# A transformer block pair on one core: the triangular inversion keeps one running matrix, and GpSimd's weight remainders come in two halves

## Chip, core and metric

The kernel runs on one core of a Trainium2 chip. What is measured is the time of one launch on the device, in microseconds (us). Before the change the median of three runs is 1421.59 us (1421.49 to 1422.59).

## What is computed

Two transformer blocks follow each other on a sequence of 512 tokens and 1024 features, in float32. The part that the change touches is in the first block: a gated delta rule, in chunks. The reference has chunks of 64; the kernel works in four chunks of 128 tokens and four heads, which is mathematically the same. Per chunk and head it needs the inverse of a unit lower triangular matrix:

```
lower = where(causal_strict, (k * beta) @ k.T * decay, 0)
tmat  = inverse(eye + lower)
u, w  = tmat @ (v * beta), tmat @ (k * beta * exp(gc))
```

The other part is in every dense product of both blocks (`w_in`, `w_out`, gate, up, down and so on): weights and activations are float32, and each product is made of reduced-precision pieces, as the next section says.

## The kernel before

**Dense products.** A weight block of 128 x 1024 values (`WB`) is loaded by the SP queue into one of three `raw` buffers. ScalarE casts it to the rounded high part `wh` (line 2128), and GpSimd subtracts, `wl = raw - wh`, in one instruction of 128 x 1024 (line 1780), which raises `wl_ready` by one. A product tile is `gemm` (lines 1794 to 1825): per 128 rows of weights, called a k below, three matmuls of 128 x 512: high weight by high activation (1818), low by high (1819), high by low (1820). `gemm` waits for the block's `wl_ready` before its first matmul. `gemm_pair` and `gemm_triple` work on two and three tiles at once (lines 1827 to 1871), and `by_token` (line 953, through `pe_tile`) does products by token; all wait for `wl_ready` too, and so does SP before it loads a `raw` buffer again (line 1754). `gemm(..., part=(i, n))` does only the i-th n-th of a tile's eight k, so that a tile can be spread over other work.

**The inversion.** For each chunk, `U` holds the strictly upper triangular matrix of four heads (the transpose of `lower`). The inverse is built by doubling: at level `lev` (0 to 6) the blocks of size m = 2^lev on the diagonal are known, and pairs of them are joined to blocks of 2m. `Y` is the running inverse and `X` its transpose. `UM` is `U` times a mask that leaves only the blocks that this level joins. At each level from 1 on:

1. TensorE makes P = UM^T X (line 2020), four heads, for each of two chunks (e = 0, 1).
2. ScalarE copies P out to `PS` (line 2294).
3. TensorE makes the update of X from Y and PS (line 2030; not at the last level) and the update of Y from PS and Y (line 2033).
4. VectorE subtracts both: X at line 2615, Y at line 2616.

The four chunks are done as two pairs, one after the other. Each of these float32 matmuls of 128 x 128 x 128 is two instructions in the trace, so that one of steps 1 or 3 for both chunks is 16 instructions; a TensorE transpose of 128 x 128 is one instruction. VectorE makes the `UM` of the next level (line 2601) after this level's P, and in the first pair one head of `qg` per level (line 2606). Before P of every level TensorE does a third of one of the tiles cc0, cc1, cb0, cb1 (`INV_FILL`; three, three and two k), and at levels 3 and 6, where a tile is complete, VectorE reads it (`cc_tile`, `cb_tile`, lines 2553 to 2567) ahead of the subtractions. Level 0 has no matmuls but transposes of UM (line 2015), and VectorE's steps 2579, 2581, 2585 and 2591.

After the inversion comes the scan over the chunks, whose first matmul (line 2052) waits for all of `Y`. While the inversion runs, GpSimd also computes the pooling branch (`multiscale`), once `qg` has its fourth head.

```
gemm(*INV_FILL[pair, lev][0], part=(INV_FILL[pair, lev][1], 3))
for h in range(H):
    last = nc.tensor.matmul(auxh[2 * e][:, h, :], UM[:, e, h, :], X[:, e, h, :], start=True, stop=True)
```

Of the kernel before, what the change touches and what calls it, by code (L numbers as in the profile page):

```python
# [7 lines left out]
F32 = mybir.dt.float32  # L8
# [3 lines left out]
ALU = mybir.AluOpType  # L12
# [199 lines left out]
def build(nc, ins, out):  # L212
    pl = Plan()
    with ExitStack() as ctx:
# [268 lines left out]
        um_ready = signal("um_ready")  # L483
        p_ps = signal("p_ps")
# [141 lines left out]
        INV_PAIR = 2 * LEVELS  # L626

# [310 lines left out]
        def tensor_second(pe, gemm, gemm_pair, ssq, transpose4, mlp, state):  # L938
# [29 lines left out]
            def pe_tile(pe, kind, idx):  # L968
# [3 lines left out]
                pe.wait_ge(wl_ready, pl.tiles[t][2] + 1)  # L972
# [772 lines left out]
        def _(sp):  # L1745
# [3 lines left out]
            for b in range(len(pl.blocks)):  # L1749
                if b == RAW:  # L1750
                    parameters(sp)
                if b >= RAW:

                    sp.wait_ge(wl_ready, b - RAW + 1)
# [5 lines left out]
        def _(pool):  # L1760
# [15 lines left out]
            for b in range(len(pl.blocks)):  # L1776
# [3 lines left out]
                nc.gpsimd.tensor_tensor(wl[pl.slot[b]][:, 0:w], raw[b % RAW][:, 0:w],  # L1780
                                        wh[pl.slot[b]][:, 0:w].bitcast(F32), ALU.subtract).then_inc(wl_ready, 1)
# [10 lines left out]
        def _(pe):  # L1792
            state = dict(t=0)

            def gemm(kind, idx, mov=None, ready=None, order=None, part=None, into=None):
# [5 lines left out]
                pe.wait_ge(wl_ready, b + 1)  # L1801
# [9 lines left out]
                for n, k in enumerate(order or range(nk)):  # L1811
# [5 lines left out]
                    c = k * stride + col  # L1817
                    nc.tensor.matmul(ps, h[:, c:c + P], mh[:, k, :], start=(n == 0), stop=False)  # L1818
# [5 lines left out]
            def gemm_triple(first, fill):  # L1824
# [3 lines left out]
                for u in range(3):  # L1828
                    assert pl.tiles[t + u][:2] == (first[0], (first[1][0], first[1][1] + u))
                    pe.wait_ge(wl_ready, pl.tiles[t + u][2] + 1)  # L1830
# [18 lines left out]
            def gemm_pair(first, second, ready, order=None, between={}):  # L1849
# [4 lines left out]
                pe.wait_ge(wl_ready, pl.tiles[t + 1][2] + 1)  # L1854
# [145 lines left out]
            for pair in range(2):  # L2000
                for lev in range(LEVELS):
                    n0 = INV_PAIR * pair + 2 * lev
                    m0 = (INV_PAIR - 2) * pair + 2 * (lev - 1)
                    if lev > 0:
                        gemm(*INV_FILL[pair, lev][0], part=(INV_FILL[pair, lev][1], 3))
                    for e in range(2):
                        pe.wait_ge(um_ready, n0 + e + 1)
# [10 lines left out]
                        pe.wait_ge(xy_ready, n0 + e - 1)  # L2018
                        for h in range(H):
                            last = nc.tensor.matmul(auxh[2 * e][:, h, :], UM[:, e, h, :], X[:, e, h, :],  # L2020
                                                    start=True, stop=True)
                        last.then_inc(p_ps, 1)
                    if lev == 0:
                        continue
                    for e in range(2):
                        pe.wait_ge(p_ready, m0 + e + 1)
                        c = 2 * pair + e
                        if lev < LEVELS - 1:
                            for h in range(H):
                                nc.tensor.matmul(auxh[2 * e + 1][:, h, :], Y[:, c, h, :], PS[:, e, h, :],  # L2030
                                                 start=True, stop=True)
                        for h in range(H):
                            last = nc.tensor.matmul(auxh[2 * e][:, h, :], PS[:, e, h, :], Y[:, c, h, :],  # L2033
                                                    start=True, stop=True)
# [655 lines left out]
```

## Time and profile before

| what | value |
|---|---|
| median of three runs | 1421.59 us |
| the profiled execution, its own time | 1421.18 us |
| its span, first to last instruction | 1419.3 us |
| TensorE busy (matmuls) | 1342.7 us, 95% |
| VectorE, ScalarE, GpSimd busy | 47%, 37%, 37% |
| chain that ended last | TensorE 87%, VectorE 8%, ScalarE 3%, GpSimd 1% |
| granted TensorE clock, mean | 0.977 of 2.4 GHz |
| the inversion (levels 1 to 6, both pairs) | about 166 to 258 us of the span |

"PE" is TensorE's matmuls and "PEld" its weight loads, DVE is VectorE, ACT ScalarE, POOL GpSimd. The span is 1.9 us less than the time of the same execution. Matmuls overlap each other, so that the duration of one (0.28 us for a 128 x 128 one) is longer than the distance between two starts; the working below goes by distances. Most of the time goes to the dense products; the inversion takes some 6.5% of the span.

### The profile page before, as it was taken

How to read it: one execution, taken by the hardware profiler on the slowest of the kernel's cores; microseconds unless marked ns; L12 is line 12 of the kernel's file. 1: busy time of each engine (PE TensorE's matmuls, PEld its weight loads, DVE VectorE, ACT ScalarE, POOL GpSimd, SP SyncE). 2: the span in 40 equal slices, each digit the busy share in tenths (PEclk: the TensorE clock that was granted, in tenths of full speed). 3: DMA queues.
4: the chain of work that ended last, by engine and by line, in shares of the span. 5: the costliest groups of instructions: out<-in, count | busy, mean ns of one | idle time of the engine just before them, and what ended most of it. 6: DMA issues, size and time to landing. Idle time of an engine off the chain costs nothing.

```text
span 1419.3 us, 15760 instructions
## 1 busy us (share of the span) xinstructions
PE 1342.7 (95%) x6273; PEld 1075.8 (76%) x6273; DVE 661.7 (47%) x863; ACT 518.2 (37%) x785; POOL 520.5 (37%) x229
## 2 busy tenths in 40 slices
PE   4899989999999999999999999889989999999997
PEld 3677888868888888888887875555668888888885
DVE  6548876345512642212157645556568523415223
ACT  4566211253422221222254533455435423323232
POOL 2233250124444444454443432211225444444440
PEclk7899999999999999999999999999999999999998
DMA  5222210123333333333233222010114333333321
GB/s 171 60 60 74 60 30 17 30 60 111 94 100 96 98 96 97 100 94 97 83 111 82 71 78 60 30 45 30 39 54 117 104 89 104 90 104 89 104 60 60
DMA packets 211360, 111.66 MB, mean 79 GB/s; under 512 B 16140, under 2 KB 209496, under 8 KB 211288
## 3 DMA queue, kind: packets, MB, share of 16 engines
q1 hardware_dynamic: 210488, 109.81, 27.1%
q8 instruction: 50, 0.82, 0.2%
q10 hardware_dynamic: 672, 0.79, 0.2%
q14 instruction: 22, 0.18, 0.0%
q0 software_dynamic: 128, 0.07, 0.0%
HBM read 108.55 MB, written 2.10 MB: 78 GB/s over the span
## 4 chain that ended last, share of the span: by engine, by line
PE 87%; DVE 8%; ACT 3%; issue 1%; POOL 1%; DMA 0%; DVEq 0%; ACTq 0%; SPq 0%
PE bank L1818 22%; PE bank L1820 22%; PE bank L1819 22%; PE aux L2020 2%; PE aux L2033 1%; PE aux L2030 1%; PE bank L1866 1%; PE bank L1868 1%; PE bank L1867 1%; PE bank L1085 1%; PE aux L1101 1%; PE aux L1026 1%; PE aux L1014 1%; PE bank L963 1%; PE aux L1818 1%
## 5 line engine op out<-in xcount | busy, mean ns | idle before, releaser
L1780 POOL TENSOR_TENSOR wl<-raw,wh 128x1024 fp32r<-128x1024 f32 (+1 forms) x202 | 498.2, 2468 | 829.7 <-ACT wh L2128 829.6
L1818 PE MATMUL bank<-ah,wh 128*128 128x512 f32 x912 | 363.2, 398 | 0.0
L1820 PE MATMUL bank<-al,wh 128*128 128x512 f32 x912 | 356.5, 391 | 0.0
L1819 PE MATMUL bank<-ah,wl 128*128 128x512 f32 x912 | 356.3, 391 | 0.0
L2128 ACT CAST wh<-raw 128x1024 fp32r<-128x1024 f32 (+1 forms) x202 | 209.2, 1038 | 368.3 <-PE bank L1820 358.6
L1818 PEld LDWEIGHTS bank<-ah,wh 128*128 128x128 f32 x912 | 172.1, 189 | 40.0 <-issue 5.3
L1820 PEld LDWEIGHTS bank<-al,wh 128*128 128x128 f32 x912 | 171.9, 188 | 36.6
L1819 PEld LDWEIGHTS bank<-ah,wl 128*128 128x128 f32 x912 | 172.2, 189 | 35.7 <-issue 1.2
L1818 PE MATMUL bank<-yh,wh 128*128 128x512 f32 x496 | 193.8, 391 | 0.1
L1820 PE MATMUL bank<-yl,wh 128*128 128x512 f32 x496 | 193.1, 389 | 0.0
L1819 PE MATMUL bank<-yh,wl 128*128 128x512 f32 x496 | 193.0, 389 | 0.0
L1818 PEld LDWEIGHTS bank<-yh,wh 128*128 128x128 f32 x496 | 93.1, 188 | 19.7 <-DVE yl L2386 0.6
L1820 PEld LDWEIGHTS bank<-yl,wh 128*128 128x128 f32 x496 | 93.1, 188 | 19.5
L1819 PEld LDWEIGHTS bank<-yh,wl 128*128 128x128 f32 x496 | 93.1, 188 | 19.0
L1699 DVE CAST yh<-y 128x512 fp32r<-128x512 f32 x32 | 65.7, 2053 | 74.0 <-ACT y L1419 73.9
L852 DVE TENSOR_TENSOR y<-bank,sg 128x512 f32<-128x512 f32 x22 | 15.2, 692 | 162.4 <-PE bank L1820 158.6
L1714 DVE TENSOR_TENSOR acc<-bank,acc 128x512 f32<-128x512 f32 x24 | 16.6, 692 | 103.5 <-PE bank L1820 103.5
L894 DVE TENSOR_TENSOR x<-bank,x 128x512 f32<-128x512 f32 x24 | 16.6, 692 | 93.2 <-PE bank L1820 93.2
L1415 ACT ACTIVATE rl<-bank 128x512 f32<-128x512 f32 x32 | 19.1, 596 | 90.8 <-PE bank L1820 88.8
L2394 DVE TENSOR_TENSOR rstd<-rstd,sq 128x512 f32<-128x512 f32 x36 | 49.4, 1372 | 5.3 <-ACT sq L2161 4.9
L783 ACT ACTIVATE sg<-bank 128x512 f32<-128x512 f32 x22 | 13.1, 597 | 94.4 <-PE bank L1820 90.1
L2466 DVE SCALAR_TENSOR_TENSOR cc<-craw,par,cc 128x512 f32<-128x512 f32 x36 | 41.1, 1150 | 11.6 <-ACT cc L2209 10.7
(402 smaller groups left out, 1660.0 us busy)
## 6 DMA issues: line engine op xcount, KB each, us to landing
raw<-in_w_up SPq DMA_DIRECT2D x54, 512.0 KB, 4.0
raw<-in_w_down SPq DMA_DIRECT2D x48, 512.0 KB, 4.1
raw<-in_w_in SPq DMA_DIRECT2D x40, 512.0 KB, 3.9
raw<-in_w_gate SPq DMA_DIRECT2D x22, 512.0 KB, 3.8
raw<-in_w_out SPq DMA_DIRECT2D x16, 512.0 KB, 3.5
raw<-in_ple_gate SPq DMA_DIRECT2D x8, 512.0 KB, 3.7
raw<-in_w_down SPq DMA_DIRECT2D x8, 384.0 KB, 3.4
xtok<-in_x SPq DMA_DIRECT2D x4, 512.0 KB, 5.1
```

The lines of the kernel that those rows point to most:

```text
L894: freed(nc.vector.tensor_tensor(x[:, m, :], ps, x[:, m, :], ALU.add))
L1415: tile("up2", (c, j), lambda ps: nc.scalar.activation(rl[:, :], ps, ACT.Relu))
L1699: link(nc.vector.tensor_copy(yh[c % 2][:, j, :], y))
L1714: freed(nc.vector.tensor_tensor(acc[:, m, :], ps, acc[:, m, :], ALU.add))
L1780: nc.gpsimd.tensor_tensor(wl[pl.slot[b]][:, 0:w], raw[b % RAW][:, 0:w], wh[pl.slot[b]][:, 0:w].bitcast(F32), ALU.subtract).then_inc(wl_rea ...
L1818: nc.tensor.matmul(ps, h[:, c:c + P], mh[:, k, :], start=(n == 0), stop=False)
L1819: nc.tensor.matmul(ps, l[:, c:c + P], mh[:, k, :], start=False, stop=False)
L1820: last = nc.tensor.matmul(ps, h[:, c:c + P], ml[:, k, :], start=False, stop=(n == nk - 1))
L2020: last = nc.tensor.matmul(auxh[2 * e][:, h, :], UM[:, e, h, :], X[:, e, h, :], start=True, stop=True)
L2128: nc.scalar.copy(wh[pl.slot[b]][:, 0:w], raw[b % RAW][:, 0:w]).then_inc(wh_ready, 1)
L2394: nc.vector.tensor_tensor(rstd[:, :], rstd[:, :], sq[:, k % 2, :], ALU.add).then_inc(sum_ready, 1)
L2466: i = nc.vector.scalar_tensor_tensor(c[:, :], r[:, tap:tap + T], g_of("conv_qkv", 12 * tap + conv_tile(j)), c[:, :], ALU.mult, ALU.add)
```

## The change

Four things are changed.

1. In the inversion, X is no longer updated by its own matmuls. After VectorE has updated Y, TensorE transposes Y (`yt_ps`), and ScalarE copies the result out as the new X (`yt_ready`). This is done at levels 1 to 5.
2. At levels 5 and 6 (`BLOCKED = 5`) P and the update of Y are computed on sub-blocks alone: two of 32 x 32 per head at level 5, one of 64 x 64 at level 6. `U` is read without a mask there, so `UM` is not made for levels 5 and 6; copies and subtractions cover the sub-blocks alone too, level 5 in two instructions for one. The contraction still runs over 128 partitions.
3. The piece of filling product per level is cut in two, in sixths of a tile: one before P, the other after the update of Y (levels 1 to 4) or before it (levels 5 and 6).
4. GpSimd's subtraction is made in two instructions of 512 columns, each with its signal. `gemm` waits for the first alone, and for the second from the first column in the second half on; all others wait for both.

```diff
+        BLOCKED = 5
+        UM_PAIR, XT_PAIR = 2 * BLOCKED, 2 * (LEVELS - 2)
+        def halves(lev):
+            m = 1 << lev
+            return [(slice(b, b + m), slice(b + m, b + 2 * m)) for b in range(0, P, 2 * m)]
...
@@ SP, ahead of the load of block b; gemm_pair, gemm_triple and pe_tile in the same way
-                    sp.wait_ge(wl_ready, b - RAW + 1)
+                    sp.wait_ge(wl_ready, 2 * (b - RAW + 1))
...
@@ GpSimd
-                nc.gpsimd.tensor_tensor(wl[pl.slot[b]][:, 0:w], raw[b % RAW][:, 0:w],
-                                        wh[pl.slot[b]][:, 0:w].bitcast(F32), ALU.subtract).then_inc(wl_ready, 1)
+                for half in (slice(0, w // 2), slice(w // 2, w)):
+                    nc.gpsimd.tensor_tensor(wl[pl.slot[b]][:, half], raw[b % RAW][:, half],
+                                            wh[pl.slot[b]][:, half].bitcast(F32), ALU.subtract).then_inc(wl_ready, 1)
...
@@ TensorE, gemm
-                pe.wait_ge(wl_ready, b + 1)
+                pe.wait_ge(wl_ready, 2 * b + 1)
+                whole = False
...
+                    if c >= block_cols(b) // 2 and not whole:
+                        pe.wait_ge(wl_ready, 2 * (b + 1))
+                        whole = True
...
@@ TensorE, the inversion
                     if lev > 0:
-                        gemm(*INV_FILL[pair, lev][0], part=(INV_FILL[pair, lev][1], 3))
+                        fill, third = INV_FILL[pair, lev]
+                        gemm(*fill, part=(2 * third, 6))
                     for e in range(2):
-                        pe.wait_ge(um_ready, n0 + e + 1)
+                        if lev < BLOCKED:
+                            pe.wait_ge(um_ready, UM_PAIR * pair + 2 * lev + e + 1)
...
-                        pe.wait_ge(xy_ready, n0 + e - 1)
+                        if lev == 1:
+                            pe.wait_ge(xy_ready, n0 + e - 1)
+                        else:
+                            pe.wait_ge(yt_ready, XT_PAIR * pair + 2 * (lev - 2) + e + 1)
                         for h in range(H):
-                            last = nc.tensor.matmul(auxh[2 * e][:, h, :], UM[:, e, h, :], X[:, e, h, :],
-                                                    start=True, stop=True)
+                            if lev < BLOCKED:
+                                last = nc.tensor.matmul(auxh[2 * e][:, h, :], UM[:, e, h, :], X[:, e, h, :],
+                                                        start=True, stop=True)
+                                continue
+                            for even, odd in halves(lev):
+                                last = nc.tensor.matmul(auxh[2 * e][odd, h, even], U[:, 2 * pair + e, h, odd],
+                                                        X[:, e, h, even], start=True, stop=True)
                         last.then_inc(p_ps, 1)
...
+                    if lev >= BLOCKED:
+                        gemm(*fill, part=(2 * third + 1, 6))
                     for e in range(2):
                         pe.wait_ge(p_ready, m0 + e + 1)
                         c = 2 * pair + e
-                        if lev < LEVELS - 1:
+                        for h in range(H):
+                            if lev < BLOCKED:
+                                last = nc.tensor.matmul(auxh[2 * e][:, h, :], PS[:, e, h, :], Y[:, c, h, :],
+                                                        start=True, stop=True)
+                                continue
+                            for even, odd in halves(lev):
+                                last = nc.tensor.matmul(auxh[2 * e][even, h, odd], PS[:, e, h, even],
+                                                        Y[:, c, h, odd], start=True, stop=True)
+                        last.then_inc(xy_ps, 1)
+                    if lev < BLOCKED:
+                        gemm(*fill, part=(2 * third + 1, 6))
+                    if lev < LEVELS - 1:
+                        for e in range(2):
+                            pe.wait_ge(xy_ready, n0 + e + 1)
                             for h in range(H):
-                                nc.tensor.matmul(auxh[2 * e + 1][:, h, :], Y[:, c, h, :], PS[:, e, h, :],
-                                                 start=True, stop=True)
-                        for h in range(H):
-                            last = nc.tensor.matmul(auxh[2 * e][:, h, :], PS[:, e, h, :], Y[:, c, h, :],
-                                                    start=True, stop=True)
-                        last.then_inc(xy_ps, 1)
+                                last = nc.tensor.transpose(auxh[2 * e + 1][:, h, :], Y[:, 2 * pair + e, h, :], ident)
+                            last.then_inc(yt_ps, 1)
...
@@ ScalarE, per level
-                        nc.scalar.copy(PS[:, e], auxh[2 * e][:, :, :]).then_inc(p_ready, 1)
+                        if lev < BLOCKED:
+                            i = nc.scalar.copy(PS[:, e], auxh[2 * e][:, :, :])
+                        else:
+                            for even, odd in halves(lev):
+                                i = nc.scalar.copy(PS[odd, e, :, even], auxh[2 * e][odd, :, even])
+                        i.then_inc(p_ready, 1)
+                    if lev < LEVELS - 1:
+                        for e in range(2):
+                            act.wait_ge(yt_ps, XT_PAIR * pair + 2 * (lev - 1) + e + 1)
+                            nc.scalar.copy(X[:, e], auxh[2 * e + 1][:, :, :]).then_inc(yt_ready, 1)
...
@@ VectorE, per level
-                    if lev < LEVELS - 1:
+                    if lev < BLOCKED - 1:
...
-                        if lev < LEVELS - 1:
-                            nc.vector.tensor_tensor(X[:, e], X[:, e], auxh[2 * e + 1][:, :, :], ALU.subtract)
-                        nc.vector.tensor_tensor(Y[:, c], Y[:, c], auxh[2 * e][:, :, :], ALU.subtract).then_inc(
-                            xy_ready, 1)
+                        for even, odd in halves(lev) if lev >= BLOCKED else [(slice(0, P), slice(0, P))]:
+                            i = nc.vector.tensor_tensor(Y[even, c, :, odd], Y[even, c, :, odd], auxh[2 * e][even, :, odd],
+                                                        ALU.subtract)
+                        i.then_inc(xy_ready, 1)
```

## Rows read from the trace of the kernel before

**Rows 1.** The page: span, busy shares, and the chain's shares by engine.

```profile
span 1419.3 us, 15760 instructions
...
PE 1342.7 (95%) x6273; PEld 1075.8 (76%) x6273; DVE 661.7 (47%) x863; ACT 518.2 (37%) x785; POOL 520.5 (37%) x229
...
PE 87%; DVE 8%; ACT 3%; issue 1%; POOL 1%; DMA 0%; DVEq 0%; ACTq 0%; SPq 0%
```

**Rows 2.** Busy by stretch: inversion, change of pair (stretch, length, engines, PEclk, DMA).

```profile
165.00:260.00 95.00, 87.53 (x650) 82.15 (x651) 64.43 (x92) 18.32 (x29) 24.48 (x18) 0.96 0.08 23
...
203.00:217.00 14.00, 9.82 (x54) 8.53 (x53) 8.73 (x11) 2.12 (x3) 6.57 (x5) 0.76 0.14 38
```

**Rows 3.** Timeline of one level, first pair, level 2 (start, us, engine, line).

```profile
173.65 1.98 PEld L2020 LDWEIGHTS aux<-X,UM 128*128 128x128 f32 x16
...
174.96 0.58 ACT L2294 COPY PS<-aux 128x512 f32<-128x512 f32 x1 [5.98 <-PE aux L2020]
...
175.60 0.97 PEld L2030 LDWEIGHTS aux<-PS,Y 128*128 128x128 f32 x8
...
176.49 0.97 PEld L2033 LDWEIGHTS aux<-Y,PS 128*128 128x128 f32 x8
...
179.17 0.19 PEld L1818 LDWEIGHTS bank<-ah,wh 128*128 128x128 f32 x1
...
180.15 0.68 DVE L2616 TENSOR_TENSOR Y<-Y,aux 128x512 f32<-128x512 f32 x1
...
180.44 1.98 PEld L2020 LDWEIGHTS aux<-X,UM 128*128 128x128 f32 x16
```

**Rows 4.** The chain of waits: eight full transposes, one filling matmul.

```profile
132.38 0.87 PE aux L1892 x8
...
186.23 0.23 PE bank L1818
```

**Rows 5.** Timeline: the narrowest weights and shortest moving operands of the trace.

```profile
792.50 1.05 PE L945 MATMUL aux<-ones,nrow 1*128 1x1 f32 x8
...
814.84 0.32 PEld L982 LDWEIGHTS aux<-cst,c 4*128 4x128 f32 x4 [0.35 <-issue]
...
989.47 0.20 PEld L1101 LDWEIGHTS aux<-pT,vt 128*64 128x64 f32 x4 [0.37 <-issue]
...
989.84 0.19 PEld L1818 LDWEIGHTS aux<-ah,wh 128*128 128x128 f32 x1 [0.17 <-issue]
```

**Rows 6.** The chain of waits: change of pair, and the inversion's end.

```profile
206.31 0.69 DVE Y L2616
...
207.66 2.72 DVE Y L2581
...
211.04 1.11 PE aux L2015 x4
212.16 0.43 PE bank L1818
...
216.00 2.08 PE aux L2020 x16
...
258.32 1.16 PE aux L2052 x8
```

**Rows 7.** Timeline: VectorE beside GpSimd's subtraction, ahead of the first P.

```profile
160.36 0.69 DVE L2581 TENSOR_TENSOR Y<-cst,UM 128x512 f32<-128x512 f32 x1
...
161.02 2.88 POOL L1780 TENSOR_TENSOR wl<-raw,wh 128x1024 fp32r<-128x1024 f32 x1 [6.67 <-ACT wh L2128]
161.69 2.77 DVE L2581 TENSOR_TENSOR Y<-cst,UM 128x512 f32<-128x512 f32 x1
...
166.30 1.86 PEld L2020 LDWEIGHTS aux<-X,UM 128*128 128x128 f32 x16 [2.29 <-DVE UM L2591]
```

**Rows 8.** Line 1780 alone: duration min/median/max ns; the chain's stop at it.

```profile
L1780 POOL TENSOR_TENSOR wl<-raw,wh x202: 1835/2392/2947, 19.4 to 1381.7; 128x1024 fp32r<-128x1024 f32 x97, 128x768 fp32r<-128x768 f32 x4
...
811.03 4.74 POOL wl L1780 x2
```

More of the change, by code:

```diff
@@ L483, in build @@
         um_ready = signal("um_ready")
+        yt_ps = signal("yt_ps")
+        yt_ready = signal("yt_ready")
         p_ps = signal("p_ps")
@@ L971, in pe_tile @@
                 state["t"] += 1
-                pe.wait_ge(wl_ready, pl.tiles[t][2] + 1)
+                pe.wait_ge(wl_ready, 2 * (pl.tiles[t][2] + 1))
                 eng, n = pl.read[t - NBANK]
@@ L1829, in gemm_triple @@
                     assert pl.tiles[t + u][:2] == (first[0], (first[1][0], first[1][1] + u))
-                    pe.wait_ge(wl_ready, pl.tiles[t + u][2] + 1)
+                    pe.wait_ge(wl_ready, 2 * (pl.tiles[t + u][2] + 1))
                     eng, n = pl.read[t + u - NBANK]
@@ L1853, in gemm_pair @@
                 assert (pl.tiles[t][:2], pl.tiles[t + 1][:2]) == (first, second)
-                pe.wait_ge(wl_ready, pl.tiles[t + 1][2] + 1)
+                pe.wait_ge(wl_ready, 2 * (pl.tiles[t + 1][2] + 1))
                 if t >= NBANK:
@@ L2577, in _ @@
                             dve.wait_ge(p_ps, INV_PAIR - 2)
+                            dve.wait_ge(yt_ps, XT_PAIR)
+                            dve.wait_ge(yt_ready, XT_PAIR)
                         for e in range(2):
                             nc.vector.tensor_tensor(UM[:, e], U[:, 2 * pair + e], mask, ALU.mult).then_inc(um_ready, 1)
-                            dve.wait_ge(um_ready, n0 + e + 1)
+                            dve.wait_ge(um_ready, UM_PAIR * pair + e + 1)
                             nc.vector.tensor_tensor(Y[:, 2 * pair + e], over_heads(ident), UM[:, e], ALU.subtract)
```

## The prediction

> **What bounds the kernel now.** I read the page's busy shares and its chain first: TensorE is busy 95% of the span and holds 87% of the chain, VectorE 8% [rows 1]. So the dense products, which the change does not shorten, go at TensorE's pace. Next the busy time by stretch: in the 95 us of the inversion TensorE is busy 92%, and where the pairs change (203 to 217 us) its granted clock averages 0.76 [rows 2]. Then the timeline of one level [rows 3]: P, the two updates and the filling product follow one another on TensorE with hardly a gap, from 173.65 to 180.44. ScalarE's copy (0.58) and VectorE's subtractions lie beside them. The inversion is thus bound by the number of TensorE's instructions, except at the change of pair, where VectorE makes the new UM, Y and X.
>
> **Prices.** One step of 16 instructions takes 1.78 us, 0.111 each (175.60 to 176.49 is eight) [rows 3]. Eight full transposes take 0.87 [rows 4]. A filling matmul takes 0.23, so a k of three 0.69 [rows 4].
>
> **Levels 1 to 4, TensorE.** The X update (1.78) goes, transposes for both chunks (0.89) come: 0.89 less work per level. What is new is a serial path: Y update, VectorE, transpose, ScalarE, next P. From a level's first P (s): P ends at s+1.78; the copy of P starts about 0.3 after its last matmul issues and takes 0.6 [rows 3], so the Y update runs from s+1.84 to s+3.63. VectorE's subtraction of the first chunk starts 0.35 after its matmuls, at s+3.1, and takes 0.65; transposes could start at s+3.8, second chunk s+4.65. TensorE meanwhile does the second piece of filling product, one k to s+4.32 or two to s+5.0, so the transposes wait for nothing (with qg on VectorE in the first pair, 0.2). ScalarE's copy of X needs 0.95 after the first chunk's transposes; 0.45 of the second chunk's and at least 0.69 of filling cover it. So a level takes 5.9 with two k until the next P and 6.6 with three. Before it took 6.8 and 7.5. If one k were missing, 0.3 would show.
>
> **Level 3 is the exception.** There the filling tile is complete only in the second piece, at s+4.32, and VectorE reads it (cc_tile or cb_tile) ahead of its subtractions. So the first transposes wait for 0.35 of signal, 0.7 of tile and 0.65 of subtraction: s+6.05, a stall of 1.7, and the second chunk 0.15 more. Level 3 takes 8.5 with its two k up to the next P; the saving is gone there, twice. In the second pair VectorE's two 0.75 convolution steps go ahead of the tile, and it starts at s+4.8: the same 8.6. GpSimd's subtraction no longer falls on them, as ScalarE's cast now comes after the copies of X.
>
> **Levels 5 and 6.** No row has such a small matmul. Level 5 has 32 instructions per step (two blocks), level 6 has 16. Bounds for one: 0.114 is the pace of instructions with full weights and one column (eight in 1.05) [rows 5]; at the other end, 64-column weights and 128 moving columns in turn on two halves of the array come at 0.05 (four in 0.37 with the drain) [rows 5], and the array time of 32 columns is a quarter of the 0.111, 0.03. Between lies 0.061, the distance of four weight loads with four moving columns: (0.32 - 0.137)/3 [rows 5]. I take 0.062, since both operands are short there too and TensorE's own issue seems to set it. To this comes the change of shape: that block of four takes 0.37 where two rounds of array time are 0.21, and ahead of it stand 0.37 without a load [rows 5]; I take 0.15 per block in and out, bounds 0 and 0.5. A step of level 5 is then 2.13, against 1.78 before; of level 6, 1.15. Level 5 becomes 2.13 + 1.39 of filling + 0.15 + 2.13, transposes 0.89 with a wait of 0.3 for VectorE's four short subtractions, and 0.69: 7.85 with all; level 6 is 3.15 on TensorE and 0.8 for VectorE: 3.95.
>
> The Trainium skill (TensorEngine Tiling (Array Packing), Key Properties) says "Changing tiling mode (not just tile) drains the TensorE". The waits around the 64-column block agree with it [rows 5]; without any drain the sum would gain 1.2 us more.
>
> **Start, change of pair, end.** Ahead of the first P, VectorE's `Y` step takes 2.77 beside GpSimd's 2.88, against 0.69 without it [rows 7]. A half takes about 1.33 (1835 ns for 768 columns and 2392 for 1024 give 2.0 ns per column and 0.3 fixed [rows 8]), so the wait is at most that: P starts at 165.3 instead of 166.3. Less filling stands ahead of it, under the same wait: nothing, as TensorE idles there already. Pair 0 then takes 6.1 + 6.6 + 8.5 + 5.9 + 7.85 + 3.95 = 38.9, to 204.2 (before 40.7, to 207.0). At the change of pair GpSimd's subtraction meets VectorE again; two halves stop it twice, each time shorter: Y's 2.72 [rows 6] becomes two waits. UM, Y, UM, transposes then take 4.4, X and UM 2.6 more, and P follows, at about 211.1: 6.9 instead of 9.0, of which 1.3 is the third k, which is no longer ahead of P at the half clock (0.43 a matmul [rows 6]). Pair 1: 5.9 + 0.3 (clock) + 6.6 + 8.6 + 5.9 + 7.85 + 3.95 = 39.1, to 250.2 against 258.3 [rows 6]. The inversion gives 8.1.
>
> **Edits at no cost inside it.** ScalarE has ten copies of 0.6 more per pair; it is nearly idle there [rows 2] and the cast queued behind them feeds a block three ahead. VectorE loses ten X updates and four UM. POOL's multiscale starts at level 4 as before and is done before the next pair.
>
> **The halves elsewhere.** TensorE waits for `wl` in no `gemm`: the chain stops at line 1780 only where `by_token` waits for two blocks, 4.74 [rows 8], and that waits for both halves still. So the early signal gives 0. The second instruction costs 0.28 per block: 0.5 at 811. GpSimd has 2.6 of work per 5.5 us of a tile; SP's next load starts 0.3 later, three blocks ahead. Where VectorE has a row of operations with two operands in SBUF, port time is the same and each half stops another one: I count four such places on the chain, 0.1 to 0.3 each; together +1.0. The added wait within `gemm` queues two or more k of matmuls behind it that are not due; 0, and if TensorE's queue ran dry, 0.05 for each of some 200 tiles, 10 us: that bound lies beyond the range, and tiles today begin with two waits at no gap.
>
> **Sum.** -8.1 + 1.0 = -7.1. On the profiled execution's span of 1419.3 us that is 1412.2; its own time is 1.9 more, 1414.1, and the median was 0.4 above that execution: 1414.5.
>
> **Rivals.** *Narrow matmuls in parallel.* The four column groups work side by side and short loads are cheap, pace 0.03: the 192 instructions of the narrow steps (128 at level 5, 64 at level 6) give 192 x 0.032 = 6.1 more, less 1 for the waits on VectorE: 1409.4. For: the block at 0.05 [rows 5]; against: 0.061 with four columns. The Trainium skill (same page, Theoretical Speedup) promises up to 4x for a dimension of 32 or less; by it this case holds, and 0.061 is the row against it. Chance 0.17.
>
> *The clock falls.* TensorE idles longer at level 3 (1.7) and does little in levels 5 and 6. The 2.29 us without a load before the first P [rows 7] left the clock up (the levels after it run at 0.111 an instruction [rows 3]); some 4 us around 208 brought it to half [rows 6]. A halved stretch of 3.4 to 6.8 us costs half of itself. Two short ones per pair: 4 x 1.7 = 6.8, giving 1421.3, no difference. For: 0.76 at the change of pair [rows 2]. Chance 0.18.
>
> *Slower: narrow steps do not overlap.* Each load of a narrow block waits for the matmul before it: 0.137, the load's own duration at line 982, in place of 0.062: 192 x 0.075 = +14.4, so 1428.9. Its place is levels 5 and 6; from 0.099 on the gain is gone, from 0.114 it is slower. Against: the loads in [rows 5] are 0.05 to 0.06 apart. Chance 0.09.
>
> *A longer path.* The path through transpose and copy is 0.5 longer at each of ten levels: +5, 1419.5. It is in the range. Chance 0.1.
>
> **Numbers.** The forecast has 0.46, and its own bounds (pace 0.05 to 0.08, drains 0 to 0.5, stalls) reach from 1411 to 1418. With the rivals, 1409 to 1421 holds 8 in 10. A measurement tells 0.2%, 2.8 us, from nothing. Faster: 0.46 + 0.17 + some of the others, 0.69; same 0.20; slower 0.11.
>
> **What would show it.** The first scan matmul (line 2052) near 250; transposes after each Y update with waits only at level 3 (1.7 before them, put down to VectorE's Y); two 1.3 instructions at line 1780; weight loads of width 32 at 0.06; the distance of filling matmuls unchanged at 0.23. Wrong would be: narrow loads over 0.1 apart, PEclk at 0.5 in more stretches than the one around 208, or a wait ahead of P put down to ScalarE's X.

## The result and the profile after

The changed kernel takes **1409.61 us** (median of four runs, 1408.91 to 1410.63) against 1422.05 for the kernel before beside it: a ratio of 0.9913, 95% interval 0.9896 to 0.993. The forecast was 1414.5, in a range of 1409 to 1421, with 0.69 on faster. The sign holds, and so does the range, by 0.6 us; the forecast's own bounds without the rivals, 1411 to 1418, do not. The size is short by 4.9 us, and the value lies on that of the rival "narrow matmuls in parallel" (1409.4).

The profiled execution took 1408.91 us, 0.7 less than the median. Its page:

```profile
span 1406.8 us, 15946 instructions
...
PE 1329.6 (95%) x6257; PEld 1057.0 (75%) x6257; DVE 609.3 (43%) x839; ACT 528.6 (38%) x809; POOL 574.2 (41%) x431
...
PE 86%; DVE 8%; ACT 3%; issue 1%; POOL 1%; DMA 0%; DVEq 0%; ACTq 0%; SPq 0%
```

The same two stretches as before (stretch, length, engines, PEclk, DMA):

```profile
165.00:260.00 95.00, 86.94 (x731) 75.65 (x732) 43.73 (x73) 32.89 (x59) 26.87 (x24) 0.98 0.11 29
203.00:217.00 14.00, 12.46 (x85) 11.06 (x86) 9.68 (x13) 3.42 (x6) 4.17 (x3) 0.88 0.15 39
```

And the timeline of one level, first pair, level 2 (start, us, engine, line):

```profile
171.20 1.95 PE L2040 MATMUL aux<-X,UM 128*128 128x128 f32 x16
...
172.99 2.00 PE L2056 MATMUL aux<-Y,PS 128*128 128x128 f32 x16
...
174.40 1.38 DVE L2661 TENSOR_TENSOR Y<-Y,aux 128x512 f32<-128x512 f32 x2
...
175.99 1.03 PEld L2069 LDWEIGHTS aux<-cst,Y 128*128 128x128 f32 x8
176.22 1.04 PE L2069 MATMUL aux<-cst,Y 128*128 128x128 f32 x8
176.85 1.07 ACT L2338 COPY X<-aux 128x512 f32<-128x512 f32 x2 [3.08 <-PE aux L2069]
```

Against [rows 2, 3]: VectorE's busy time in the stretch falls from 64.4 to 43.7 us (in both pairs together twenty X updates and eight UM are gone, and the collisions with GpSimd are shorter), ScalarE's rises by 14.6 (it copies X). The level goes P (171.20), Y update (172.99), filling, transposes (176.22), filling, and the transposes wait for nothing: the subtractions at 174.40 end before they are due.

Levels 5 and 6 of the first pair, and what follows at the change of pair (the chain of waits of the changed kernel: start, us, what):

```profile
192.16 0.63 PE aux L2044 x32
192.79 0.44 PE bank L1832
...
195.51 1.26 PE aux L2069 x8
...
197.47 1.07 PE aux L2044 x16
...
199.48 0.63 DVE cin L2600
...
200.96 0.83 DVE UM L2625
201.81 0.69 DVE Y L2627
202.50 0.63 DVE UM L2625
203.15 1.65 DVE Y L2627
204.80 1.20 DVE X L2631 x2
206.00 1.73 DVE UM L2637
207.78 2.05 PE aux L2040 x16
...
243.80 1.16 PE aux L2087 x8
```

Here is the surprise: a step of level 5, 32 instructions, takes 0.63 us, where the forecast had 2.13. Level 6, with 16, takes 1.07. The product behind a step of level 5 stands in the chain with 0.44 instead of 0.23, so part of the step's cost is there. The timeline gives the loads by themselves: level 3's stall at the transposes, level 5's first step and its wait at the transposes, and level 6's first step.

```profile
183.63 0.42 PEld L2069 LDWEIGHTS aux<-cst,Y 128*128 128x128 f32 x4 [1.81 <-DVE Y L2661]
...
192.09 0.59 PEld L2044 LDWEIGHTS aux<-X,U 128*32 128x32 f32 x32 [0.36 <-issue]
...
195.51 0.42 PEld L2069 LDWEIGHTS aux<-cst,Y 128*128 128x128 f32 x4 [0.60 <-DVE Y L2661]
...
197.40 1.01 PEld L2044 LDWEIGHTS aux<-X,U 128*64 128x64 f32 x16 [0.36 <-ACT X L2338]
```

The scan's first product starts at 243.80 instead of 258.32 [rows 6], 14.5 us earlier; the end is 12.5 earlier. Setting the dense products of the two traces side by side, one by one, 1.6 us of it are lost between 781 and 784 us of the changed kernel, where its clock was granted at half for 6.8 us and that of the kernel before, at the same work, for 3.4. Two stretches that begin at the same work, 17 us each, columns as above: first the changed kernel's, then that of the kernel before.

```profile
774.00:791.00 17.00, 17.00 (x83) 12.47 (x82) 15.62 (x20) 4.53 (x6) 7.71 (x6) 0.80 0.42 120
```

```profile
787.00:804.00 17.00, 17.00 (x92) 13.48 (x90) 16.31 (x20) 5.74 (x7) 7.57 (x3) 0.90 0.43 115
```

A granted clock of 0.80 against 0.90 over 17 us is 1.7 us of TensorE's work.

### The profile page after: what moved, and what is told of

It reads as the page before. It is cut to its first block, busy times and chain, and to the rows that moved or that the text cites. A ratio compares the mean times of both kernels' runs of the same rounds, so it can differ in the third digit from the quotient of the medians.

```text
span 1406.8 us, 15946 instructions
## 1 busy us (share of the span) xinstructions
PE 1329.6 (95%) x6257; PEld 1057.0 (75%) x6257; DVE 609.3 (43%) x839; ACT 528.6 (38%) x809; POOL 574.2 (41%) x431
## 4 chain that ended last, share of the span: by engine, by line
PE 86%; DVE 8%; ACT 3%; issue 1%; POOL 1%; DMA 0%; DVEq 0%; ACTq 0%; SPq 0%
PE bank L1832 22%; PE bank L1834 22%; PE bank L1833 22%; PE aux L2040 1%; PE bank L1880 1%; PE aux L2056 1%; PE bank L1882 1%; PE bank L1881 1%; PE bank L1094 1%; PE aux L1110 1%; PE aux L2069 1%; PE aux L1035 1%; PE bank L972 1%; PE aux L1023 1%; PE aux L1832 1%
## 5 line engine op out<-in xcount | busy, mean ns | idle before, releaser
L1790 POOL TENSOR_TENSOR wl<-raw,wh 128x512 fp32r<-128x512 f32 (+1 forms) x404 | 552.2, 1389 | 769.1 <-ACT wh L2163 769.0
L1832 PEld LDWEIGHTS bank<-yh,wh 128*128 128x128 f32 x496 | 93.1, 188 | 19.5 <-DVE yl L2430 0.5
L1834 PEld LDWEIGHTS bank<-yl,wh 128*128 128x128 f32 x496 | 93.1, 188 | 19.5
L1708 DVE CAST yh<-y 128x512 fp32r<-128x512 f32 x32 | 34.8, 1086 | 77.7 <-ACT y L1428 77.7
L1709 DVE TENSOR_TENSOR yl<-y,yh 128x512 fp32r<-128x512 f32 x32 | 52.2, 1630 | 1.1
L2510 DVE SCALAR_TENSOR_TENSOR cc<-craw,par,cc 128x512 f32<-128x512 f32 x36 | 36.2, 1014 | 14.1 <-ACT cc L2244 13.3
```

The lines of the kernel that those rows point to most:

```text
L1708: link(nc.vector.tensor_copy(yh[c % 2][:, j, :], y))
L1709: nc.vector.tensor_tensor(yl[c % 2][:, j, :], y, yh[c % 2][:, j, :].bitcast(F32), ALU.subtract).then_inc(y_ready[1], 1)
L1790: nc.gpsimd.tensor_tensor(wl[pl.slot[b]][:, half], raw[b % RAW][:, half], wh[pl.slot[b]][:, half].bitcast(F32), ALU.subtract).then_inc(wl_ ...
L1834: last = nc.tensor.matmul(ps, h[:, c:c + P], ml[:, k, :], start=False, stop=(n == nk - 1))
L2510: i = nc.vector.scalar_tensor_tensor(c[:, :], r[:, tap:tap + T], g_of("conv_qkv", 12 * tap + conv_tile(j)), c[:, :], ALU.mult, ALU.add)
```

## How the runs were read: the clock

The executions of one kernel differ by up to 6.7 us (early2), and the mean granted clock that each lists differs too (0.975 to 0.98 in early). At 1405 us, 0.001 of it is 1.4 us. So beside the median each experiment has a second number: span times mean granted clock, averaged over its runs, minus the same for the kernel before beside it. That is the difference if TensorE had kept its full clock, as far as TensorE is the bound; the clock is listed to three digits, and the products of single executions scatter by 0.3 to 3.2 us (most in later), so it is good to 1 or 2 us. For the first run of the changed kernel the clocks beside it are not on record. The third is the stretch from the first P to the scan's first product in the profile, which is the inversion.

| kernel | median us | ratio to before (95%) | at full clock, us | first P to scan, us |
|---|---|---|---|---|
| before | 1422.05 to 1423.85 | 1 | 0 | 92.0 |
| changed, first | 1409.61 | 0.9913 (0.9896 to 0.993) | not known | 78.6 |
| same (changed, again) | 1407.09 | 0.9893 (0.9877 to 0.991) | -13.1 | 80.1 |
| whole | 1413.0 | 0.993 (0.9917 to 0.9944) | -11.3 | 79.9 |
| halves | 1419.54 | 0.9972 (0.9961 to 0.9984) | -2.2 | 90.8 |
| inside | 1409.22 | 0.9905 (0.9892 to 0.9919) | -14.2 | 78.6 |
| outside | 1413.82 | 0.9934 (0.9922 to 0.9947) | -10.7 | 79.9 |
| noblocks | 1419.55 | 0.9971 (0.9959 to 0.9982) | -6.3 | 88.0 |
| six | 1416.82 | 0.9955 (0.9942 to 0.9969) | -10.4 | 83.7 |
| groups | 1409.57 | 0.9909 (0.9894 to 0.9924) | -12.8 | 79.1 |
| twice | 1409.73 | 0.991 (0.9896 to 0.9925) | -13.4 | 80.9 |
| later | 1404.44 | 0.9867 (0.9854 to 0.9881) | -18.9 | 76.5 |
| early | 1400.2 | 0.9844 (0.9828 to 0.9859) | -20.9 | 71.7 |
| early2 | 1403.53 | 0.9857 (0.984 to 0.9875) | -19.5 | 72.2 |

**same** is the changed kernel with no edit.

> The changed kernel again, unaltered, on the chip of the runs beside it, so that they can be set against it and not only against the kernel before. Ratio to the kernel before 0.991 as first measured. If the two products of the low parts with one instruction (0.993) are right, this one stands 2 to 3 us below that.

It came out at 0.9893. Set against the first profile of the same code, its dense products are 2.2 us behind after the change of pair (where the clock was down when P ran), level (0.3) at 797 us and 2.1 ahead at 939. That is how far one execution can be trusted.

## The experiments on the sub-blocks

**noblocks** has full products at levels 5 and 6 too, the filling order kept:

```diff
-        BLOCKED = 5
+        BLOCKED = 7
...
```

> The changed kernel with full 128x128 products at levels 5 and 6 as well (UM made for them by VectorE), filling order kept. By the trace of the changed kernel a step takes 0.63 at level 5 and 1.07 at level 6 against 1.78 for a full one: 4 x 1.15 + 4 x 0.71 = 7.4 us more than the changed kernel if TensorE alone bounds these levels, some 8 to 9 if the copy and the longer subtractions show as well: 1417 to 1418.5. If the short steps only move the wait to VectorE and ScalarE (rival), 3 to 5 us more. By the prediction on record (0.062 an instruction) it would be 4 x (1.78 - 2.13) + 4 x (1.78 - 1.15) = 1.1 us more only.

Measured: 9.4 us more from the first P to the scan (88.0 against 78.6), 6.8 to 7.9 at full clock. By level, from P to P in both pairs: level 5 takes 7.15 and 7.14 (5.31 twice with the sub-blocks), level 6 with what follows 2.6 and 1.6 more. And 1.4 us is neither: level 4 takes 6.95 and 6.35 instead of 5.97 twice. VectorE now makes a UM for level 5 while GpSimd subtracts, and the transposes wait for it (timeline of noblocks, level 4 of the first pair; engine, line, releaser):

```profile
186.25 2.94 POOL L1790 TENSOR_TENSOR wl<-raw,wh 128x512 fp32r<-128x512 f32 x2 [22.02 <-ACT wh L2163]
...
186.91 2.82 DVE L2647 TENSOR_TENSOR UM<-U,cst 128x512 f32<-128x512 f32 x2 [3.03 <-PE aux L2040]
...
190.98 0.42 PEld L2069 LDWEIGHTS aux<-cst,Y 128*128 128x128 f32 x4 [1.12 <-DVE Y L2661]
```

The two UM take 1.3 us where nothing collides. The forecast had booked the UM left out as "no cost"; by noblocks and six it is worth 1.4.

**six** has the sub-blocks at level 6 only (`BLOCKED = 6`, order kept), so that level 5's own worth shows.

> The changed kernel with short products at level 6 only, full ones at level 5. By the prediction on record (a level 5 step of 2.13 against 1.78) this would be 1.4 us faster than the changed kernel. By the pace found since (0.63 a step): 4 x 1.15 = 4.6 us slower, plus what VectorE's and ScalarE's longer pieces show, less the 0.6 of wait at the transposes that full products cover: 4.5 to 6 us more than the changed kernel.

Measured: 5.1 us more in the stretch (83.7 against 78.6), of which 3.9 at level 5 itself (7.24 twice) and 1.4 at level 4, as above; 7.6 in the median against inside, which ran beside it; the clock has 3.3 of that (mean 0.9732 against 0.9755), and at full clock 3.8 are left. The expected 4.5 to 6 is met by the stretch and lies between the other two. The forecast's own pace for level 5 would have made this kernel faster. It falls by a wide margin.

**twice** issues every short product of level 5 twice.

```diff
-                            for even, odd in halves(lev):
+                            for even, odd in halves(lev) * (7 - lev):
...
```

> The changed kernel with every short product of level 5 issued twice in a row of blocks (128 more instructions, the same values). It prices them on the path. Theory A (0.016 each as the trace has it): 128 x 0.016 = 2.0 us more, steps of about 1.15. Rival B (the instructions are cheap only in a short burst, from a queue that has been filled ahead): the second half of each step comes at 0.03 to 0.06, steps of 1.6 to 2.6, 4 to 8 us more. The prediction on record (0.062) would have 7.9.

The first step's loads in the timeline of twice:

```profile
192.37 1.09 PEld L2044 LDWEIGHTS aux<-X,U 128*32 128x32 f32 x64 [0.36 <-issue]
```

64 loads in 1.09 where 32 took 0.59: the further 32 cost 0.50, 0.0156 each, and hold no burst effect (rival B is out). From level 5's P to level 6's it takes 6.07, 0.77 more: 1.0 of products, less 0.25 of the wait at the transposes, which was 0.60 and is now 0.35. That is 1.5 in both pairs. The stretch grows by 2.3, mostly for the first level of the second pair, which took 7.01 instead of 5.98 beside a halved clock. The times alone would not show it (13.4 us below the kernel before at full clock, against 13.1 and 14.2 for the changed kernel).

**groups** puts level 5's products in the order of the blocks, all heads of one and then all heads of the other (the same in both steps; shortened).

```diff
-                        for h in range(H):
-                            for even, odd in halves(lev):
+                            for even, odd in halves(lev):
+                                for h in range(H):
...
```

> The changed kernel with the short products of level 5 in another order: all heads of the first block, then all heads of the second, so that successive instructions stay in one group of array columns. Theory A (0.016 an instruction comes from two blocks that work side by side in different rows and columns of the array): the pace goes to about 0.03, a step of level 5 from 0.63 to 1.0 to 1.2, 4 steps: 1.5 to 2.3 us more than the changed kernel. Rival B (0.016 is just what so short an instruction takes, whatever its neighbour): no difference, steps of 0.63.

The same row of groups:

```profile
191.74 0.79 PEld L2045 LDWEIGHTS aux<-X,U 128*32 128x32 f32 x32 [0.36 <-issue]
```

0.79 instead of 0.59, 0.025 each (both rows include the last load's own 0.113; from start to start it is 0.022 against 0.015): theory A in kind, less in size (level 5 takes 5.65 and 5.64 against 5.31, 0.7 us in all; 1.5 to 2.3 expected). The single starts tell why. In the changed kernel the loads come in pairs 6 to 7 ns apart, one of each block, and the pairs follow each other every 32 ns. In groups each block's loads also come every 32 ns, but the second block starts at 191.895, before the first is through at 191.956: TensorE still overlaps the ends. So one group of array columns takes an instruction every 0.032 us, and two groups run beside each other. (A block's group of columns and the partitions that its output goes to change together here, so which of the two sets the pace is not separated.) Level 6 has one block, with nothing beside it, and comes at 0.058, about half of the 0.111 of a full instruction [rows 3].

The Trainium skill (TensorE: Matmul & The Clock Gate, Part 3: Packing small matmuls — row/col tiling) says that matmuls at distinct tile positions of the array run at the same time, their starts about 4 ns apart, and that the start partition of the output picks the column tile. The trace agrees in kind; here the starts are 6 to 7 ns apart. The same skill (TensorEngine Tiling (Array Packing), Instruction Overhead) says that a matmul has an overhead of about 60 cycles, that free dimensions of 1 and 60 take the same time, and that one shouldn't take the factor from a dimension that is already small. Both operands are short here, and 64 against 32 moving columns of f32 took 0.058 against 0.032: down to 32 columns the time still falls, and the measurement decides. Whether it stops falling below that, no run here shows.

## The experiments on the halves

**halves** is the kernel before with the low parts in two halves, as in the change, and nothing else; **whole** is the changed kernel without them (one instruction that raises the semaphore by 2). The edit of whole:

```diff
-                for half in (slice(0, w // 2), slice(w // 2, w)):
-                    nc.gpsimd.tensor_tensor(wl[pl.slot[b]][:, half], raw[b % RAW][:, half],
-                                            wh[pl.slot[b]][:, half].bitcast(F32), ALU.subtract).then_inc(wl_ready, 1)
+                nc.gpsimd.tensor_tensor(wl[pl.slot[b]][:, 0:w], raw[b % RAW][:, 0:w],
+                                        wh[pl.slot[b]][:, 0:w].bitcast(F32), ALU.subtract).then_inc(wl_ready, 2)
```

> The kernel before, with the low parts in two halves and nothing else. Theory A: costs 0.5 (by 811 us, where two blocks are waited for) to 2 us over the kernel before, so 1422.5 to 1424; first P at 165.3 instead of 166.3 but no gain behind it. Rival B: the halves give time where VectorE stood behind one long subtraction (change of pair, first P): 1 to 2 us less than the kernel before, about 1420.5. The prediction on record had +1.0 outside the inversion and -1 to -2 inside it.

> The change's inversion alone: the low parts again in one GpSimd instruction that raises the semaphore by two. Theory A (the halves cost what the trace after the inversion lost, 14.5 us gained at the scan's first product and 12.5 left at the end): about 1 to 2 us less than the changed kernel, some 1408. Rival B (the 2 us lost later come from where the clock falls, not from the halves): within 0.5 us of the changed kernel, with the slower products at about 780 us still there. Rival C (the halves also gave time within the inversion by stopping VectorE for shorter at the change of pair): 1 to 2 us more, P of the second pair at 209 or later instead of 207.8.

Both say that the halves help: halves alone 0.9972 (2.2 us at full clock), and whole is behind the changed kernel by 3.4 to 5.9 us in the median, 1.8 to 2.9 at full clock (against same and inside). Two rows of VectorE and GpSimd ahead of the first P, of the changed kernel and then of outside (one instruction at this place, as before), show where:

```profile
161.47 3.03 POOL L1790 TENSOR_TENSOR wl<-raw,wh 128x512 fp32r<-128x512 f32 x2 [5.83 <-ACT wh L2163]
161.70 1.66 DVE L2627 TENSOR_TENSOR Y<-cst,UM 128x512 f32<-128x512 f32 x1
```

```profile
163.26 2.86 POOL L1790 TENSOR_TENSOR wl<-raw,wh 128x1024 fp32r<-128x1024 f32 x1 [6.69 <-ACT wh L2164]
163.91 2.75 DVE L2628 TENSOR_TENSOR Y<-cst,UM 128x512 f32<-128x512 f32 x1
```

Y takes 1.66 instead of 2.75 (2.77 before [rows 7]), so P comes 1.1 earlier behind the same product: 165.21 against a product at 162.14, whole 166.98 against 162.81. The run halves has the same 1.1 there (3.10 from that product to P instead of 4.21).

At the change of pair the halves give nothing. There VectorE has two operations behind each other that read two operands in SBUF, and each half stops one of them. In the timeline of halves:

```profile
207.13 3.39 POOL L1781 TENSOR_TENSOR wl<-raw,wh 128x512 fp32r<-128x512 f32 x2
207.76 1.64 DVE L2586 TENSOR_TENSOR Y<-cst,UM 128x512 f32<-128x512 f32 x1
...
209.32 1.74 DVE L2584 TENSOR_TENSOR UM<-U,cst 128x512 f32<-128x512 f32 x1
```

Together 3.38, against 2.72 and 0.68 before, and from level 6's P to the next P it takes 13.4 in both kernels. The second 1.1 of the run halves is at level 3 of the second pair, 7.60 instead of 8.69 from P to P: VectorE's two convolution steps met GpSimd's subtraction there (the kernel before, then halves).

```profile
233.49 3.52 DVE L2564 SCALAR_TENSOR_TENSOR convd<-cin,par,convd 128x512 f32<-128x512 f32 x2
```

```profile
233.47 2.43 DVE L2569 SCALAR_TENSOR_TENSOR convd<-cin,par,convd 128x512 f32<-128x512 f32 x2
```

In the changed kernel they no longer meet (0.76 each), with halves or without. So rival B of halves is right on the first P and wrong on the change of pair.

**inside** and **outside** divide the halves by time: up to the block made at 245 us, and from there on.

```diff
-                for half in (slice(0, w // 2), slice(w // 2, w)):
+                for half in (slice(0, w // 2), slice(w // 2, w)) if b < 24 else (slice(0, w),):
...
```

> The changed kernel with the low parts in two halves for the first 24 blocks only (those made before the scan starts, at about 245 us), in one instruction behind. Theory A (the halves earn their time at the first P and at the change of pair, and are free elsewhere): as the changed kernel, 0.989 to 0.991 of the kernel before. Rival B (they earn part of it after the inversion): 1 to 3 us more than the changed kernel. The prediction on record had them cost 1.0 us outside the inversion, which would put this one 1.0 below the changed kernel.

> The opposite: one instruction for the first 24 blocks, halves from there on. Theory A: as the changed inversion with whole low parts (0.993 of the kernel before, +2.3 us in the waits of the inversion, P of the second pair near 209 to 210). Rival B: 1 to 3 us less than that.

Inside is the changed kernel again (0.9905 between its 0.9893 and 0.9913), outside is whole again (0.9934 and 0.993). The halves earn all they earn before the scan. What they cost behind it is too small for the times, whose intervals are 2 us to either side. The traces, product by product, show it: from the scan to the end the changed kernel falls 0.2 us further behind inside (0.23, then 0.45), and outside 0.5 behind whole (1.55, then 2.02); 0.2 to 0.3 of each is the wait for two blocks. So the +1.0 of the forecast was 0.2 to 0.5. Line 1790 shows the extra instruction (row of the changed kernel), 0.2 us more per block by the medians (2 x 1294 ns against 2392):

```profile
L1790 POOL TENSOR_TENSOR wl<-raw,wh x404: 1008/1294/2087, 19.9 to 1370.5; 128x512 fp32r<-128x512 f32 x130, 128x384 fp32r<-128x384 f32 x5
```

What stays open: inside and outside are 4.6 us apart in the median and 3.5 at full clock. The profiles account for 1.1 (first P) less 0.2 (at the change of pair, 10.37 against 10.14 from P to P; VectorE's two UM there take 2.40 beside the second half and 2.25 beside one whole), and for 1.6 where P of the second pair ran at the halved clock (7.56 us from it to the next P in outside, 5.99 in inside). Whether that clock follows from the halves or only fell so in these executions was not settled: same and later, with halves, had it too (7.56 and 7.57). A further 2.4 us between the two profiles were there before the inversion (1.7 of it at the first dense product, 28 us into the span); the remaining 2 us of the median are not explained.

## The experiments on what is left

**later** takes VectorE's tile of level 3 from ahead of its two subtractions of Y to behind them.

```diff
-                    if INV_FILL[pair, lev][1] == 2:
+                    if INV_FILL[pair, lev][1] == 2 and lev == LEVELS - 1:
...
+                    if INV_FILL[pair, lev][1] == 2 and lev < LEVELS - 1:
+                        kind, t = INV_FILL[pair, lev][0]
+                        (cc_tile if kind == "cc" else cb_tile)(t)
```

> The changed kernel with the VectorE tile of level 3 (cc or cb) put behind VectorE's two subtractions of Y instead of ahead of them. Theory A (the wait of 1.8 to 2.0 at the transposes of level 3 is this order): the wait goes, level 3 takes about 6.6 instead of 8.3 to 8.5, twice: 3 to 3.7 us less, if the tile is not needed sooner by anyone: 1406 to 1407. Rival B: the tile, now late, delays VectorE's next work (qg or the UM of level 4), so that 1 to 2 us of it comes back as a wait at level 4: 1 to 2 us less. Rival C: the time is taken back by the clock later: no difference at the end though the scan starts 3 us earlier.

Level 3 of the first pair in the timeline of later:

```profile
180.86 1.28 DVE L2661 TENSOR_TENSOR Y<-Y,aux 128x512 f32<-128x512 f32 x2
181.60 1.01 PEld L2069 LDWEIGHTS aux<-cst,Y 128*128 128x128 f32 x8
...
182.06 0.68 DVE L2600 TENSOR_TENSOR cin<-bank,cin 128x512 f32<-128x512 f32 x1
```

The transposes at 181.60 wait for nothing, and level 3 takes 6.58 in both pairs instead of 8.33 and 8.50: 3.7 us, as theory A has it, and no later wait takes them back. In the profile 1.6 went to the clock at the change of pair (P there took 2.94 instead of 2.05).

**early** has that edit, and lets VectorE make the second pair's UM and Y behind its level 5 of the first. UM is free there, since the short products read U: the change itself made that room. The transposes' wait for the last Y goes, as they touch nothing of it.

```diff
...
+                    if pair == 0 and lev == BLOCKED:
+                        start_pair(1)
```

> Two edits on the changed kernel: the level 3 tile behind the subtractions, as in the run named later (measured 0.9867 of the kernel before); and the second pair's UM and Y made by VectorE behind its level 5 of the first pair, where UM lies unused since the short products read U itself, with the wait of the transposes for the last Y taken out, as nothing of theirs is read by it. Theory A (at the change of pair TensorE waits for this chain on VectorE: 1.4 + 0.7 at the transposes and 2.5 at P): 3.9 us of VectorE go from the chain, P of the second pair starts at about 201 to 202 instead of 205.8, so 3.5 to 5 us less than that run: 1400 on this chip. Rival B (ScalarE's or GpSimd's work becomes the next wait, or the clock falls as before): 1 to 2 us less. Rival C: the filling product runs out of a weight block that now comes too late, so no difference.

The change of pair in the timeline of early:

```profile
199.57 1.09 PE L2029 MATMUL aux<-cst,UM 128*128 128x128 f32 x8
...
201.15 1.27 DVE L2635 TENSOR_TENSOR X<-cst,aux 128x512 f32<-128x512 f32 x2
202.34 1.28 DVE L2641 TENSOR_TENSOR UM<-U,cst 128x512 f32<-128x512 f32 x2
```

From level 6's P to the second pair's first P it takes 6.55 instead of 10.4. 3.9 us are gained, the transposes follow the Y update at once, and PEclk in the stretch from 203 to 217 is 1.00 instead of 0.88. The next level gives 0.65 back (6.64 instead of 5.99): GpSimd's subtraction now falls on its two UM, which take 3.00, and the transposes wait. So 3.2 stay. At 0.9844 this kernel is the fastest of all in the median, ahead of both the kernel before and the changed one; its interval touches that of later, and at full clock 2.0 lie between the two. UM and Y cost VectorE 4.65 us there instead of the 2.8 that they take undisturbed, because GpSimd's multiscale reads beside them; it has the time.

**early2** moves two things more on VectorE (the tile of level 6 behind X and UM; X, UM, X, UM).

> The run named early (0.9844 of the kernel before) with two moves more on VectorE: the tile of level 6 of the first pair behind the second pair's X and UM instead of ahead of its Y subtraction, and X, UM, X, UM instead of X, X, UM, UM. Theory A (VectorE's chain to the second pair's first P is the bound there): 0.69 for the tile and 0.64 for the order, 1.0 to 1.4 us less. Rival B (the tile's bank comes free later and the filling product waits for it, or P's second chunk waits for what the first no longer does): 0 to 0.5 less.

P comes 0.7 sooner (5.84 after level 6's), but its second chunk now waits, and the level behind it takes 7.06 instead of 6.64, in the first pair 6.71 instead of 5.99. The stretch is 72.2 against 71.7: no gain, as rival B has it: what the first chunk wins, the second waits for. A miss.

## Why the forecast was right in sign and short in size

- **Levels 1, 2 and 4**: 5.9, 6.6 and 5.9 forecast, 5.99, 6.58 and 5.97 measured. The X update gone, transposes in its place, the serial path covered by filling: right. The rival "a longer path" (+5) is out.
- **Level 3**: 8.5 and 8.6 forecast with a stall of 1.7 and 0.15; 8.33 and 8.50 with 1.81 and 0.18. Right, with its cause, which later removed.
- **Level 5 is the step that failed.** The forecast took 0.062 per instruction, "since both operands are short there too and TensorE's own issue seems to set it", from four loads with four moving columns [rows 5], and 2.13 per step. Measured: 0.0185 by the loads' row (0.59 over 32), 0.0156 for each one added, 0.63 per step. A level 5 took 5.31, not 7.85 (its terms as written add up to 7.7): 5.1 us of the 6.4 by which the inversion came out shorter (14.5 against 8.1). The row read has weights 128 columns wide (4 x 128), so it had no neighbouring group for another instruction; that this is why it stands at 0.061 is argued and not tested. The nearer row was the other bound, the 64-column weights "in turn on two halves of the array": its single loads start in pairs 5 to 6 ns apart, as those of level 5 do. With two pairs alone that row gives no pace, but it showed two groups side by side. The array time of 32 columns, 0.03, stood in the same paragraph and was right for each group of columns; that two groups run beside each other was missing. The wait at the transposes was 0.60, not 0.3.
- **Level 6**: 1.15 per step forecast, 1.07 measured; 3.95 against 3.6 and 3.7. Right, so the rival "in parallel" was right on the total and on level 5 (it even asked too little there) and wrong on level 6: it reached 1409.4 by two errors that cancel, 0.03 instead of 0.016 for 128 instructions and 0.03 instead of 0.058 for 64.
- **Start and change of pair**: P at 165.3 and 6.9 from pair to pair; 165.21 and 6.75. Right. The 1.1 behind the same product is what counts of the first: in the other profiles of this code P starts between 164.9 and 166.6. The worth of UM left out (1.4 at level 4) was booked at nothing, and it is inside the levels' own times above, which were worked out without that collision.
- **The halves elsewhere**, +1.0: 0.2 to 0.5. The profile's 2.0 between the scan's start and the end is 1.6 of clock near 780 us and 0.3 in the wait for two blocks, which takes 5.04 instead of 4.74 [rows 8]. That the end came nearer to the forecast (5.4 us of span) than the inversion did (6.4) is luck: a clock that the forecast did not have stands where its +1.0 stood.
- **"The clock falls"**: it fell for less at the change of pair (0.88 against 0.76), and for more near 780. Out as a term of 6.8; in a single execution it is worth 1 to 3 us either way.
- **"Narrow steps do not overlap"**: loads of 106 to 138 ns start 6 and 25 ns apart in turn at level 5, 58 at level 6. Out.

## What to carry to other kernels

Price a short matmul by the array time of its columns and count how many column groups its neighbours can occupy, and issue neighbours from different groups alternately. After such a change look at what it freed, not only at what it shortened: here the buffer UM lay idle for two levels, and using it early was worth 3.9 us, a quarter of what the change brought to the inversion, and 3.2 after what the next level gave back. Where two engines read SBUF together, cutting one long instruction in two pays only where the other stands on the chain, and there only if the second half finds no second such operation to stop.

## What was not expected of the hardware

- An f32 instruction with 128x32 weights and 32 moving columns took 0.032 us in one group of columns and 0.016 with a second group alternating; with 64 and 64 it took 0.058, with 128 and 128 0.111.
- Around a block of short products about 0.34 us is lost: at level 5 the step and the first product behind it stand in the chain with 0.63 and 0.44, where 32 x 0.0156 and a usual product are 0.73; at level 6 with 1.07 and 0.43, where 16 x 0.058 and 0.23 are 1.16. The forecast had 0.15.
- VectorE's operation with two operands in SBUF waited for the whole of GpSimd's instruction that had started before it (2.75 beside 2.86) and only for the half of it where there were two (1.66). At the change of pair two operations took 2.40 beside the second half, and 2.25 beside the whole one (in outside). Operations with one operand in PSUM took their usual 0.68 beside GpSimd's.
- The halved clock is not bound to the code: the same kernel had it at 780 us in one profile and not in the next.
